# Half of the preceding item's down product between steps six and seven of gate and up, in an expert loop on one core

## The chip, the cores and the metric

One core of a Trainium2 chip runs the whole block. The metric is the device time of one execution in microseconds, lower is better; a kernel's time is the median of its runs. The profile is of one execution of its own.

## The reference

The reference is a decoder block: two attention branches that share one input projection, a gated merge, and then a sparse expert layer. The expert layer is what matters here:

```python
logits = (t @ w_router) + b_router          # 512 tokens, 32 experts
top_val, top_idx = lax.top_k(logits, 4)
gate = jax.nn.softmax(top_val, axis=-1)
# for each block of rows xb that chose expert e:
gu = xb @ w_gate_up[e] + b_gate_up[e]       # 1024 -> 2048
g, u = gu[:, :1024], gu[:, 1024:]
g = jnp.minimum(g, 7.0); u = jnp.clip(u, -7.0, 7.0)
a = (u + 1.0) * (g * jax.nn.sigmoid(1.702 * g))
y = a @ w_down[e] + b_down[e]               # 1024 -> 1024, times the gate, summed per token
```

Everything is float32. Each expert has 8 MB of gate and up weights and 4 MB of down weights.

## The kernel before

The first 420 us or so compute both attention branches, the merge and the routing. The rest is the expert layer, and the change lies there. An expert's rows make one **item**. Experts are ranked by how many tokens chose them: even items (0, 2, ..., 30) take up to 96 rows in 3 groups of 32, odd items up to 64 rows in 2 groups. The trace has 32 items. Item 0 and the last, item 31, stand outside the loop; a hardware loop `with pe.Fori(0, n_pairs) as pair` runs 15 times and does an odd item (`i` = 1) and an even item (`i` = 2) each time. I call one turn of it a **pair**.

Weights stream from HBM. SyncE issues six transfers of 2 MB for each item, in this order: gate and up in four parts, each for two of the eight steps (`gu_head` holds the first three parts, for steps 0 to 5, `gu_tail` the fourth, for steps 6 and 7), then down in two halves (`dn_even`, or `dn_odd0` and `dn_odd1`). There is one buffer for each gate and up part, so a part of the next item is only issued when TensorE is through with that part of this one (`gu_used`, and for the fourth part `bank_done`); the down weights have two sets of buffers, taken in turn, and each half is issued when the same half of the down product two items before is done (`dn_used`).

TensorE does for each item, in program order:

- `gate_up(i)` (L1816 to L1841): waits for `xT_ready` (the item's rows, transposed and scaled by VectorE) and for `gu_out` (VectorE has emptied the PSUM banks of the item before), then eight steps `k`, each waiting for its weights at even `k`, 4 products of 512 columns for each group (L1824). In even items the sums of earlier outputs into tokens (`pair_sums`, L1790) stand behind steps 1, 3, 5 and 6, and the first of them waits for `y_kept`.
- `lists(i + 2)` (L1770): a few small products for the token list of a later item.
- `down(i - 1)` (L1856 to L1874): the down product of the **preceding** item, in two halves `j`. It waits for `a_ready` (VectorE has written the activations `aT`) and `y_kept` (VectorE has taken the last down product out of PSUM).

A float32 product of the program stands as two matmul records in the trace: a half of an even item's down product is 16 + 8 products, 48 records.

VectorE's program order in each turn is fixed as well, and the prediction rests on it:

```python
pick(i + 2, later, pair)
if i == 2:
    for c in range(NB):
        add_sums(c, pair * 4 + (c + 1))
turn_out(i, pair)          # L1295: PSUM of gate and up -> act_gu
turn_rows(i + 1, pair)     # L1283, L1287: the next item's xT, then xT_ready
index(i + 2, pair)
keep_gates(i + 2, pair)
activate(i, e, pair)       # L1304 to L1314: ends in aT, a_ready
keep_low(i - 1, pair)      # L1323: y_lo, then y_kept
```

`turn_out` can only begin when `gate_up(i)` has filled a bank, at its last step. So between the end of `gate_up(i)` and the start of `gate_up(i + 1)`, VectorE empties PSUM and transposes the next item's rows, and TensorE does `lists` and `down(i - 1)`. GpSimd fetches the rows of a later item by an indirect DMA (L685) and ScalarE does the sigmoid (L905) and the first part of the output (`y_hi`, L912).

Of the kernel before, what the change touches and what calls it, by code (L numbers as in the profile page):

```python
# [56 lines left out]
def hybrid_block(nc, x, positions, norm1_g, w_in, b_forget, b_gate, q_norm_swa, k_norm_swa, sinks,  # L57
# [41 lines left out]
    with ExitStack() as ctx:  # L99
# [247 lines left out]
        def sem(name):  # L347
            return ctx.enter_context(nc.semaphore(name))
# [53 lines left out]
        a_ready = sem("a_ready")  # L402
        dn_used = [sem(f"dn_used{j}") for j in (0, 1)]
        y_high, y_kept, put_ready = sem("y_high"), sem("y_kept"), sem("put_ready")
        sums_ps, sums_added, out_done = sem("sums_ps"), sem("sums_added"), sem("out_done")
# [4 lines left out]
        def groups(i):  # L410
            return N_GROUPS - i % 2
# [7 lines left out]
        def counted(per_pair, at, pair):  # L419
            return at if pair is None else pair * per_pair + at  # L420
# [4 lines left out]
        def dn_chunk(i, j):  # L425
            return (dn_odd0, dn_odd1)[j][:, :] if i % 2 else dn_even[:, j, :]

        def gu_columns(k, j):
            return gu_chunk(k).rearrange("p (b n) -> p b n", b=4)[:, :, j * P:(j + 1) * P]

        def rows_of(i):

            return xT_odd[:, :, :] if i % 2 else xT[:, :, 0:groups(i) * GROUP]
# [1015 lines left out]
        def _(pe):  # L1449
# [313 lines left out]
            def lists(i, pair=None):  # L1763

                pe.wait_ge(sel_ready, counted(2, i + 1, pair))
                if i > 0:
                    pe.wait_ge(idx_ready, counted(2, i, pair))
                for a in (0,) if i % 2 else (0, 1):
                    for c in range(NB):
                        ins = pe.matmul(list_v[:, a, :], sel[:, c, a, :], row_now[:, c, :], start=(c == 0), stop=(c == NB - 1))  # L1770
                ins.then_inc(list_ps, 1)
# [11 lines left out]
            def sums(parts, c, n, banks=SUM_BANKS):  # L1783

                pe.wait_ge(sums_added, n)
                for at, (table, y) in enumerate(parts):
                    for half in (y_hi[y], y_lo[y]):
                        for h in (0, 1):
                            rows = slice(h * HD, (h + 1) * HD)
                            ins = pe.matmul(ps[:, banks, :][:, h], table[rows, c * P:(c + 1) * P], half[rows, :],  # L1790
                                            start=(at == 0 and half is y_hi[y]),
                                            stop=(at == len(parts) - 1 and half is y_lo[y]))
                return ins

            def pair_sums(c, pair, banks=SUM_BANKS, added=None):

                if c == 0:
                    pe.wait_ge(y_kept, pair * 2 + 2)
                    pe.wait_ge(put_ready, pair * 3 + 3)
                ins = sums(((put_odd, 2), (put_even, 0), (put_even_b, 1)), c, pair * 4 + ((c if added is None else added) + 1), banks)  # L1800
                ins.then_inc(sums_ps, 1)

            def bias_rows(h):

                pe.wait_ge(gateT_ready, 1)
                pe.wait_ge(gates_step, 1)
                pe.wait_ge(b_dn_in, 2 * 16 * NB)
                if h == 1:
                    pe.wait_ge(bdn_out, NB)
                for c in range(NB):  # L1810
                    pe.matmul(ps[:, BIAS_BANKS[c], :], gateT[c * E:(c + 1) * E, :], b_dn[h][c * E:(c + 1) * E, :],
                              start=True, stop=True).then_inc(bdn_ps, 1)

            def gate_up(i, pair=None, last=False):

                pe.wait_ge(xT_ready, counted(2, i + 1, pair))  # L1816
                if i > 0:
                    pe.wait_ge(gu_out, counted(2, i, pair))
                for k in range(KD):
                    if k % 2 == 0:  # L1820
                        pe.wait_ge(gu_in[k // 2], counted(32, i * 16 + 16, pair))
                    for n in range(groups(i)):
                        for j in range(4):
                            ins = pe.matmul(ps[j * GROUP:(j + 1) * GROUP, n, :], rows_of(i)[:, k, n * GROUP:(n + 1) * GROUP],  # L1824
                                            gu_columns(k, j), start=(k == 0), stop=(k == KD - 1))
                        if k == KD - 1:
                            ins.then_inc(bank_done, 1)
                    if k % 2 and k < KD - 1:
                        ins.then_inc(gu_used[k // 2], 1)
                    if i == 2 and k in SUM_STEPS:  # L1830
                        pair_sums(SUM_STEPS.index(k), pair)
                    if last and k == 3:
                        down(0, pair)
                    if last and k == 5:
                        pair_sums(0, pair)
                    if last and k == 6:
                        pair_sums(1, pair, LAST_BANKS[1], added=0)
                    if i == 0 and k == 1:
                        lists(1)
                    if i == 0 and k in (2, 5):  # L1840
                        bias_rows(k // 4)  # L1841
                    if i == 0 and k == 3:
                        extras()

            def extras():

                pe.wait_ge(extra_ready, 1)
                pe.wait_ge(gates_step, 3)
                for a, col in enumerate((x_expert, x_first, x_low)):
                    ins = pe.matmul(extra_ps[:, a, :], col[:, :].broadcast_to([E, P]), eyes[0:E, :], start=True, stop=True)  # L1850
                ins.then_inc(extra_ps_done, 1)

            def down(i, pair=None):

                pe.wait_ge(a_ready, counted(2, i + 1, pair))
                pe.wait_ge(y_kept, counted(2, i + 1, pair))  # L1856
                if i == 0:
                    pe.wait_ge(sums_added, counted(4, 1, pair))
                for j in (0, 1):
                    pe.wait_ge(dn_in[i % 2][j], counted(16, i // 2 * 16 + 16, pair))  # L1860
                    for k in range(4):
                        for u in range(4):
                            ins = pe.matmul(ps[u * GROUP:(u + 1) * GROUP, 5, :],  # L1863
                                            aT[:, 4 * j + k, u % 2 * GROUP:(u % 2 + 1) * GROUP],
                                            dn_chunk(i, j)[:, k * D + u // 2 * 512:k * D + (u // 2 + 1) * 512],
                                            start=(j == 0 and k == 0), stop=(j == 1 and k == 3))
                    if i % 2 == 0:
                        for k in (0, 2):
                            for u in range(4):
                                ku = k + u % 2  # L1870
                                ins = pe.matmul(ps[u * GROUP:(u + 1) * GROUP, 4, :], aT[:, 4 * j + ku, 2 * GROUP:],  # L1871
                                                dn_chunk(i, j)[:, ku * D + u // 2 * 512:ku * D + (u // 2 + 1) * 512],
                                                start=(j == 0 and k == 0), stop=(j == 1 and k == 2))
                    ins.then_inc(dn_used[j], 1)  # L1874
# [19 lines left out]
            ins.then_inc(gates0_ps, 1)  # L1894
            keep_warm(6)
            gate_up(0)
            lists(2)
            pe.wait_ge(items_ready, 1)
            n_pairs = pe.value_load(pairs[0:1, 0:1], min_val=PAIRS, max_val=MAX_PAIRS)
            with pe.Fori(0, n_pairs) as pair:  # L1900
                for i in (1, 2):
                    gate_up(i, pair)
                    lists(i + 2, pair)
                    down(i - 1, pair)
            gate_up(1, n_pairs, last=True)
            pair_sums(2, n_pairs, added=1)
            pair_sums(3, n_pairs, LAST_BANKS[1], added=2)
            down(1, n_pairs)
            pe.wait_ge(y_kept, n_pairs * 2 + 3)
            pe.wait_ge(put_ready, n_pairs * 3 + 4)  # L1910
# [25 lines left out]
```

## Time and profile before

| what | value |
|---|---|
| median of 3 runs | 1433.8 us (1432.73 to 1436.41) |
| the profiled execution's own time | 1432.87 us |
| its span | 1430.8 us |
| TensorE (PE) busy | 1363.6 us, 95% |
| VectorE (DVE) busy | 746.7 us, 52% |
| ScalarE (ACT), GpSimd (POOL) busy | 222.5 us, 191.0 us |
| weights' DMA queue q1 | 435.96 MB |
| DMA, HBM over the span | 312 GB/s |

The span runs from the first to the last instruction on record and is 2.1 us shorter than the execution's own time. Busy time of TensorE says little about how well it is used, as its matmuls are pipelined. The mean over the span also hides that the expert loop, from 447 us on, is a stage of its own, with other limits than the attention before it. In the views by window and in the timeline, times are microseconds from the start of the span.

### The profile page before, as it was taken

Reading aid. Unit: us, or ns where it says so; the run is one execution under the profiler, and the core shown is the slowest. Engines: PE = TensorE matmul, PEld = TensorE weight load, DVE = VectorE, ACT = ScalarE, POOL = GpSimd, SP = SyncE. Lnnn points to the kernel's source line nnn. Section 1 sums busy time; section 2 is a strip of 40 time slices with the busy share of each in tenths; the row PEclk is TensorE's granted clock in tenths of the full one; section 3 lists DMA queues with packets and bytes.
Section 4 is the critical chain, followed back from the end, with each engine's and each line's share of the span. In section 5 each row is a group of like instructions: output and inputs, shape, how many; then the busy total and the mean of one; then the engine's idle time right before and its main releaser. Section 6 shows DMA issues by size and latency. Waiting matters only on the chain.

```text
span 1430.8 us, 27506 instructions
## 1 busy us (share of the span) xinstructions
PE 1363.6 (95%) x11224; PEld 645.4 (45%) x11227; DVE 746.7 (52%) x1481; ACT 222.5 (16%) x415; POOL 191.0 (13%) x242
## 2 busy tenths in 40 slices
PE   6999999999989999999999999999899999999997
PEld 5888887778953333333232322323232332323233
DVE  5213736765257575454645444564544446565444
ACT  4224426642220000000000000000000000000000
POOL 2001400000002112021120202021020202112020
PEclk9999999999999999999999999999999999999999
DMA  6231320013679999999999999999999999999992
GB/s 192 88 117 61 114 91 1 2 34 120 245 301 368 409 395 416 404 414 414 409 413 397 418 406 414 415 410 415 392 418 407 409 414 415 417 399 417 402 413 116
DMA packets 59127, 447.27 MB, mean 313 GB/s; under 512 B 8592, under 2 KB 26032, under 8 KB 34480
## 3 DMA queue, kind: packets, MB, share of 16 engines
q1 hardware_dynamic: 55904, 435.96, 76.4%
q0 software_dynamic: 3072, 10.49, 2.3%
q8 instruction: 27, 0.44, 0.1%
q10 hardware_dynamic: 112, 0.28, 0.1%
q14 instruction: 12, 0.10, 0.0%
HBM read 442.51 MB, written 4.19 MB: 312 GB/s over the span
## 4 chain that ended last, share of the span: by engine, by line
PE 73%; DMA 19%; issue 4%; DVE 2%; ACT 1%; POOL 0%; SPq 0%; DVEq 0%; POOLq 0%; ACTq 0%
PE ps L1824 31%; DMA gu_head<-in_w_gate_up_dram 11%; PE ps L1863 10%; DMA gu_tail<-in_w_gate_up_dram 7%; PE ps L1790 7%; PE ps L1483 3%; PE ps L1485 3%; PE ps L1484 3%; PE ps L1871 2%; PE ps L1508 2%; PE ps L1509 2%; PE ps L1507 2%; PE ps L1474 1%; PE ps L1476 1%; PE ps L1475 1%
## 5 line engine op out<-in xcount | busy, mean ns | idle before, releaser
L1824 PE MATMUL ps<-gu_head,xT 128*32 128x512 f32 x2304 | 257.2, 594 | 3.0 <-DMA gu_head<-in_w_gate_up_dram 3.0
L1331 DVE TENSOR_TENSOR x_tok<-x_tok,ps 128x1024 f32<-128x1024 f32 x68 | 82.7, 1221 | 255.4 <-PE ps L1790 255.4
L1824 PE MATMUL ps<-gu_head,xT_odd 128*32 128x512 f32 x1536 | 168.5, 592 | 0.8 <-DVE act_gu L1295 0.6
L905 ACT ACTIVATE act_s<-act_gu 128x768 f32<-128x768 f32 (+1 forms) x32 | 23.6, 738 | 928.2 <-DVE act_gu L1306 893.5
L1824 PEld LDWEIGHTS ps<-gu_head,xT 128*32 128x32 f32 x2304 | 70.7, 110 | 169.5 <-issue 157.1
L1295 DVE STREAM_TRANSPOSE act_gu<-ps 128x512 f32<-128x512 f32 x80 | 57.2, 715 | 137.9 <-PE ps L1824 133.1
L685 POOL DMA_INDIRECT xg<-h_dram,idx_g x32 | 70.0, 2186 | 440.8 <-DVE row_all L1264 440.8
L942 DVE TENSOR_TENSOR st_l<-st_w,st_h 128x2048 fp32r<-128x2048 f32 x25 | 57.3, 2292 | 113.5 <-ACT st_h L749 113.5
L1863 PE MATMUL ps<-dn_even,aT 128*32 128x512 f32 x1024 | 116.1, 594 | 0.0
L1863 PE MATMUL ps<-dn_odd,aT 128*32 128x512 f32 x1024 | 113.2, 594 | 2.2 <-DVE aT L1314 2.2
L1824 PEld LDWEIGHTS ps<-gu_head,xT_odd 128*32 128x32 f32 x1536 | 49.3, 110 | 116.2 <-issue 110.7
L1824 PE MATMUL ps<-gu_tail,xT_odd 128*32 128x512 f32 x512 | 66.7, 666 | 29.4 <-DMA gu_tail<-in_w_gate_up_dram 29.4
L1824 PE MATMUL ps<-gu_tail,xT 128*32 128x512 f32 x768 | 88.8, 596 | 0.0
L1283 DVE STREAM_TRANSPOSE xT<-xg 32x256 f32<-32x256 f32 x180 | 77.7, 432 | 2.3
L1863 PEld LDWEIGHTS ps<-dn_odd,aT 128*32 128x32 f32 x1024 | 31.6, 110 | 70.0 <-issue 67.0
L1863 PEld LDWEIGHTS ps<-dn_even,aT 128*32 128x32 f32 x1024 | 31.7, 110 | 68.0 <-issue 67.6
L1871 PE MATMUL ps<-dn_even,aT 128*32 128x512 f32 x512 | 60.8, 592 | 0.0
L1283 DVE STREAM_TRANSPOSE xT_odd<-xg 32x256 f32<-32x256 f32 x128 | 55.1, 431 | 1.9 <-DMA xg<-h_dram,idx_g 0.4
L713 POOL COPY put_row<-row_all 128x1 f32 x15 | 2.8, 188 | 383.7 <-PE ps L1790 383.7
L749 ACT CAST st_h<-st_w 128x2048 fp32r<-128x2048 f32 x25 | 47.6, 1903 | 32.2 <-PE ps L1509 30.3
L1824 PEld LDWEIGHTS ps<-gu_tail,xT_odd 128*32 128x32 f32 x512 | 16.8, 120 | 77.3 <-DMA gu_tail<-in_w_gate_up_dram 40.5
L1483 PE MATMUL ps<-hT_h,st_h 128*128 128x512 f32 x128 | 50.0, 391 | 0.0
(373 smaller groups left out, 2009.6 us busy)
## 6 DMA issues: line engine op xcount, KB each, us to landing
gu_head<-in_w_gate_up_dram SPq DMA_DIRECT2D x96, 2048.0 KB, 22.4
gu_tail<-in_w_gate_up_dram SPq DMA_DIRECT2D x32, 2048.0 KB, 20.5
dn_even<-in_w_down_dram SPq DMA_DIRECT2D x32, 2048.0 KB, 25.1
dn_odd<-in_w_down_dram SPq DMA_DIRECT2D x32, 2048.0 KB, 21.5
st_w<-in_w_in_dram SPq DMA_DIRECT2D x17, 1024.0 KB, 5.3
st_w<-in_w_out_dram SPq DMA_DIRECT2D x4, 1024.0 KB, 5.1
x_tok<-in_x_dram SPq DMA_DIRECT2D x4, 512.0 KB, 6.2
st_w<-in_w_o_swa_dram SPq DMA_DIRECT2D x4, 512.0 KB, 3.5
```

The lines of the kernel that those rows point to most:

```text
L685: g.indirect_dma_start(out=xg[0:n, :], out_offset=None, in_=h2_dram[:, :], in_offset=bass.IndirectOffsetOnAxis(ap=idx_g[0:n, 0:1], axis=0) ...
L749: sc.copy(st_h[:, g % 2], st_w[:, g % 2]).then_inc(split_hi, 1)
L942: v.tensor_tensor(st_l[:, g % 2], st_w[:, g % 2], st_h[:, g % 2].bitcast(F32), ALU.subtract).then_inc(split_lo, 1)
L1283: ins = v.transpose(turned_rows[r, :, s].rearrange("r (k a) s -> r k a s", a=2), near[s, r].rearrange("s p k a -> s k a p"))
L1295: ins = v.transpose(act_gu[:, :, n * GROUP:(n + 1) * GROUP].rearrange("p (b k) s -> p b k s", k=4), ps[:, n, :].rearrange("p (b r k) -> p ...
L1331: v.tensor_tensor(x_tok[:, c, :].rearrange("p (h n) -> p h n", h=2), x_tok[:, c, :].rearrange("p (h n) -> p h n", h=2), ps[:, banks, :], A ...
L1483: pe.matmul(dst, wh[:, k], xh[:, k], start=(k == 0), stop=False)
L1484: pe.matmul(dst, wh[:, k], xl[:, k], start=False, stop=False)
L1790: ins = pe.matmul(ps[:, banks, :][:, h], table[rows, c * P:(c + 1) * P], half[rows, :], start=(at == 0 and half is y_hi[y]), stop=(at == l ...
L1824: ins = pe.matmul(ps[j * GROUP:(j + 1) * GROUP, n, :], rows_of(i)[:, k, n * GROUP:(n + 1) * GROUP], gu_columns(k, j), start=(k == 0), stop ...
L1863: ins = pe.matmul(ps[u * GROUP:(u + 1) * GROUP, 5, :], aT[:, 4 * j + k, u % 2 * GROUP:(u % 2 + 1) * GROUP], dn_chunk(i, j)[:, k * D + u // ...
L1871: ins = pe.matmul(ps[u * GROUP:(u + 1) * GROUP, 4, :], aT[:, 4 * j + ku, 2 * GROUP:], dn_chunk(i, j)[:, ku * D + u // 2 * 512:ku * D + (u ...
```

## The change

The down product is cut in its two halves. Inside the loop, `down(i - 1)`'s first half (`j` = 0, with its waits for `a_ready` and `y_kept`) is called from within `gate_up(i)`, behind step 5 and ahead of step 6; the second half stays where the whole stood, behind `lists`. The item after the loop (`last`) is as it was: the whole `down(30)` behind its step 3, and `down(31)` at the end.

```diff
                     if i == 2 and k in SUM_STEPS:
                         pair_sums(SUM_STEPS.index(k), pair)
+                    if pair is not None and not last and k == 5:
+                        down(i - 1, pair, (0,))
                     if last and k == 3:
                         down(0, pair)
...
-            def down(i, pair=None):
-
-                pe.wait_ge(a_ready, counted(2, i + 1, pair))
-                pe.wait_ge(y_kept, counted(2, i + 1, pair))
-                if i == 0:
-                    pe.wait_ge(sums_added, counted(4, 1, pair))
-                for j in (0, 1):
+            def down(i, pair=None, halves=(0, 1)):
+
+                if 0 in halves:
+                    pe.wait_ge(a_ready, counted(2, i + 1, pair))
+                    pe.wait_ge(y_kept, counted(2, i + 1, pair))
+                    if i == 0:
+                        pe.wait_ge(sums_added, counted(4, 1, pair))
+                for j in halves:
                     pe.wait_ge(dn_in[i % 2][j], counted(16, i // 2 * 16 + 16, pair))
...
                     gate_up(i, pair)
                     lists(i + 2, pair)
-                    down(i - 1, pair)
+                    down(i - 1, pair, (1,))
```

On TensorE, in the odd item of a pair: the gate and up steps are L1824, the list is L1770, and the down product of the even item before is L1863 and L1871 (L1866 and L1874 in the changed kernel); the ISA rows are its waits.

```order
+L1861 ISA
+L1863 ISA
+L1866 MATMUL ps<-dn_even,aT 32x512 x16
+L1874 MATMUL ps<-dn_even,aT 32x512 x8
 L1824 MATMUL ps<-gu_tail,xT_odd 32x512 x16
 L1765 REGISTER_ALU
 L1767 REGISTER_ALU
 L1770 MATMUL ps<-row_now,sel 128x5 x4
-L1858 ISA
-L1860 ISA
-L1863 MATMUL ps<-dn_even,aT 32x512 x16
-L1871 MATMUL ps<-dn_even,aT 32x512 x8
```

The first 24 products of the down product, and both of its waits, moved from behind the list to ahead of the steps that read `gu_tail`. The next 24 follow the list in both kernels.

On TensorE, at the end of the even item of a pair, before the change (the last rows ahead of the loop's branch):

```order
L1824 MATMUL ps<-gu_tail,xT 32x512 x12
L1765 REGISTER_ALU
L1770 MATMUL ps<-row_now,sel 128x5 x8
L1863 MATMUL ps<-dn_odd_207,aT 32x512 x16
L1863 MATMUL ps<-dn_odd_206,aT 32x512 x16
```

and with the change:

```order
L1824 MATMUL ps<-gu_tail,xT 32x512 x12
L1765 REGISTER_ALU
L1770 MATMUL ps<-row_now,sel 128x5 x8
L1866 MATMUL ps<-dn_odd_206,aT 32x512 x16
```

One half of the odd item's down product is left between the end of the even item's gate and up and the start of the next odd item's; the other stands ahead of step 6, behind the third of the sums. VectorE, ScalarE, GpSimd and SyncE keep their order.

## Rows read from the trace of the kernel before

**Rows 1.** The page: busy time of the engines; the DMA share in 40 slices.
```profile
PE 1363.6 (95%) x11224; PEld 645.4 (45%) x11227; DVE 746.7 (52%) x1481; ACT 222.5 (16%) x415; POOL 191.0 (13%) x242
DMA  6231320013679999999999999999999999999992
```

**Rows 2.** The chain of waits: starts of odd items' gate and up (start, us, what).
```profile
446.94 13.94 PE ps L1824 x128
...
506.32 13.73 PE ps L1824 x128
...
565.50 13.73 PE ps L1824 x128
...
624.68 3.48 PE ps L1824 x32
...
1380.17 6.87 PE ps L1824 x64
```

**Rows 3.** Windows: length, busy time of the engines, granted clock, DMA share, GB/s.
```profile
506.30:565.50 59.20, 59.20 (x548) 19.61 (x540) 33.50 (x68) 3.32 (x5) 9.54 (x8) 1.00 1.00 405
...
1001.20:1064.00 62.80, 59.22 (x544) 19.17 (x536) 33.01 (x68) 3.32 (x5) 9.06 (x8) 1.00 1.01 408
...
1190.00:1254.40 64.40, 61.68 (x552) 19.94 (x548) 34.04 (x68) 3.32 (x5) 10.07 (x8) 0.97 1.01 414
```

**Rows 4.** Waits, 624 to 1380 us: us in total, times, longest us.
```profile
PE ps L1824 <- DMA gu_tail<-in_w_gate_up_dram: 29.4, 12, 3.2
...
PE ps L1824 <- DMA gu_head<-in_w_gate_up_dram: 3.0, 7, 0.4
```

**Rows 5.** Timeline of TensorE in one pair: start, us, instructions [idle before].
```profile
520.18 3.64 PE L1863 MATMUL ps<-dn_even,aT 128*32 128x512 f32 x32
...
525.35 3.62 PE L1863 MATMUL ps<-dn_even,aT 128*32 128x512 f32 x32
...
530.50 5.33 PE L1824 MATMUL ps<-gu_head,xT 128*32 128x512 f32 x48
...
535.76 0.50 PE L1790 MATMUL ps<-y_hi,put_odd 64*128 64x512 f32 x2
...
558.43 7.08 PE L1863 MATMUL ps<-dn_odd,aT 128*32 128x512 f32 x64
565.32 1.04 PE L1824 MATMUL ps<-gu_head,xT_odd 128*32 128x512 f32 x8
```

**Rows 6.** Timeline of VectorE in the same pair.
```profile
510.43 0.74 DVE L1323 SCALAR_TENSOR_TENSOR y_lo<-ps,gate_all,y_hi 128x512 fp32r<-128x512 f32 x1
...
520.77 5.33 DVE L1283 STREAM_TRANSPOSE xT<-xg 32x256 f32<-32x256 f32 x12
526.14 0.96 DVE L1287 TENSOR_TENSOR xT<-xT,g_near 128x768 f32<-128x768 f32 x1
...
532.26 1.41 DVE L1323 SCALAR_TENSOR_TENSOR y_lo<-ps,gate_all,y_hi 128x512 fp32r<-128x512 f32 x2
...
558.92 3.54 DVE L1283 STREAM_TRANSPOSE xT_odd<-xg 32x256 f32<-32x256 f32 x8
562.50 0.69 DVE L1287 TENSOR_TENSOR xT_odd<-xT_odd,g_near 128x512 f32<-128x512 f32 x1
```

**Rows 7.** Timeline of TensorE: three waits for `gu_tail`, and what followed.
```profile
762.91 5.34 PE L1824 MATMUL ps<-gu_tail,xT_odd 128*32 128x512 f32 x32 [3.13 <-DMA gu_tail<-in_w_gate_up_dram]
...
825.92 3.64 PE L1824 MATMUL ps<-gu_tail,xT_odd 128*32 128x512 f32 x32 [1.92 <-DMA gu_tail<-in_w_gate_up_dram]
...
888.76 5.34 PE L1824 MATMUL ps<-gu_tail,xT_odd 128*32 128x512 f32 x32 [2.70 <-DMA gu_tail<-in_w_gate_up_dram]
```

**Rows 8.** Timeline of VectorE and TensorE near the end: a wait for `y_lo`.
```profile
1420.90 0.75 DVE L1323 SCALAR_TENSOR_TENSOR y_lo<-ps,gate_all,y_hi 128x512 fp32r<-128x512 f32 x1 [5.87 <-ACT y_hi L912]
...
1421.88 0.50 PE L1790 MATMUL ps<-y_hi,put_odd 64*128 64x512 f32 x2 [1.98 <-DVE y_lo L1323]
```

**Rows 9.** Transfers of `gu_tail` from issue to landing: item 0's; the 24 from 624 us on.
```profile
DMA to landing us min/median/max: 7.6/7.6/7.6
...
DMA to landing us min/median/max: 19.0/23.1/27.4
```

## The prediction, before the changed kernel was run

> **What bounds the kernel now.** I read the page first. TensorE is busy 95% of the span, VectorE 52% [rows 1], and the DMA digits stand at 9 from the fourteenth slice to the last but one. So two resources look full in the expert loop, and the page doesn't say which one sets the pace. The chain of waits does, if one measures the distance between starts of odd items. The reader is to see that the first full pairs take 59.18 us each (506.32 to 565.50 to 624.68), and that the twelve pairs from 624.68 to 1380.17 take 62.96 us each [rows 2]. In a fast pair TensorE has no idle time at all, 59.20 us busy in a window of 59.20 us [rows 3]: 59.18 us is TensorE's own work. In the later ones it waits for weights, 29.4 us for `gu_tail` and 3.0 us for `gu_head` [rows 4]. The windows show the DMA share at 1.00 and 1.01, with 405 to 414 GB/s, in the fast pairs and in the slow ones alike [rows 3]. So the queue needs 62.96 us for a pair. At first it falls behind and lives on what was loaded ahead; from 624 us on **the queue sets the pace**, at 3.78 us a pair above TensorE's work. Over all 15 pairs TensorE would need 59.38 (the first) + 14 x 59.18 = 887.9 us. They take 933.2 us (446.94 to 1380.17). The difference, 45.3 us, is what the queue costs: 32.4 us of waits and the rest mostly a lower clock behind some of them (below).
>
> **What the change removes.** The wait for `gu_tail` in the odd item stands right where half of the even item's down product now goes, and that half lasts 5.17 us (520.18 to 525.35) [rows 5]. The waits were 3.2 us at most [rows 4]. So this wait is filled, and the drops of the clock behind it go as well. By itself this is worth little: the queue moves the same bytes in the same order and is full all the time, so a wait filled at step 6 comes back at the next transfer. It doesn't bring the queue's 62.96 us down.
>
> **What the change adds.** The whole down product used to stand between one item's gate and up and the next. Under it VectorE emptied PSUM and transposed the rows of the next item, for which the next gate and up waits. I look at what is left of that cover, in the pair at 506 us, where nothing waits for DMA.
>
> - Odd to even item. The down product begins at 520.18; half of it ends at 525.35, where the whole ended at 530.50 [rows 5]. VectorE's transposes of `xT` run from 520.77, and the scaling behind them ends at 526.14 + 0.96 = 527.10 [rows 6]. They can't come sooner: they follow `turn_out`, which needs the last step of gate and up, and their order on VectorE isn't changed. A **new wait of 1.75 us** for `xT_ready`.
> - Even item's first sums. They stand behind steps 0 and 1, 5.26 us behind the start of gate and up (530.50 to 535.76) [rows 5], so at 527.10 + 5.26 = 532.36 now. They wait for `y_kept`, and `y_lo` ends at 532.26 + 1.41 = 533.67 [rows 6]. That chain hangs on VectorE's order (the transposes, then the activations, then `keep_low`), which begins at the end of gate and up as before. A **second wait of 1.31 us**.
> - Even to odd item. The down product of the odd item takes 6.89 us (558.43 to 565.32) [rows 5]; half of it ends at 561.88. `xT_odd` is ready at 562.50 + 0.69 = 563.19 [rows 6]. A **third wait of 1.31 us**.
>
> Together 4.37 us a pair. An end on VectorE isn't a start on TensorE: `y_lo` ended at 1421.65 and TensorE began at 1421.88 [rows 8], 0.23 us later. The first wait's delay is swallowed by the second, so two of them count, each between nothing and 0.23 us; I take half, 0.25 us together. So 4.62 us a pair, with bounds of 4.37 and 4.83 from these rows. The waits could be smaller than that if VectorE ran faster beside an idle TensorE, for which no row speaks; I let them go down to 4.0.
>
> **What lies beside other work.** The first half's own waits cost nothing: in the odd item `y_lo` ends at 511.17 [rows 6], 4.85 us behind the start of gate and up at 506.32 [rows 2]; that start moves 2.1 us ahead of VectorE (half a down product of 3.45 us less the wait of 1.31 us), so 7.0 us, and six steps take 10.3 us (four take 6.87 us in the last item [rows 2]). In the last item `down(30)` stands behind four steps, 6.87 us, against those 7.0 us: 0.2 us more, once. On SyncE nothing changes its place. The reload of `gu_tail` is issued half a down product later, and the first half of the down weights right behind it, when its buffer has long been free; a transfer took 7.6 us on an empty queue [rows 9], and from the end of one gate and up to step 6 of the next there are over 20 us (3.45 + 1.3 + 10.3 + 5.17). That cover is gone only if the queue is full.
>
> **The sum.** TensorE's pace becomes 59.18 + 4.62 = 63.8 us a pair, 0.84 us above what the queue needs. So the queue's waits all go, and VectorE's take their place: 15 x 4.62 = 69.3 us come, 45.3 us go, 0.2 us at the end. Net +24.2 us. On the profiled execution's 1432.87 us that gives **1457 us**. The median shown is 0.9 us above that execution, far inside my range, and I add nothing for it.
>
> **The rivals.** A. *The queue goes on setting the pace, no change.* If VectorE's waits came to less than 3.78 us a pair, they would only fill time in which TensorE waited for weights. The pair stays at 62.96 us, and the time at 1432 to 1436 us, not slower. The point that decides is 3.78 us, and my sum is 0.84 us above it; a shorter chain on VectorE by 20% would do it. For it speaks the DMA share of 1.01 [rows 3]. The Trainium skill, page "Perfetto Trace Analysis", section "Identifying the Most-Contended Engine", says to find the most contended engine and to work on that one first, and to judge DMA by the bandwidth it reaches. By that rule DMA is the one here and a new order on TensorE would change nothing, 1433 us. Against it speaks that VectorE, at 52%, isn't loaded, yet what counts is the 6.9 us from the end of gate and up to `xT`, not its share. 11%.
>
> B. *The clock falls as well.* Behind waits of 3.13 and 2.70 us the next 32 matmuls took 5.34 us instead of 3.64 us, 1.7 us more; behind one of 1.92 us they didn't [rows 7], and the granted clock of such a window is 0.97 [rows 3]. My new waits are 1.75 us and less, but three of them stand in each pair, two of them 5.3 us apart. The Trainium skill, "TensorE: Matmul & The Clock Gate", section "What's actually happening", says that the gate goes by how busy the array has been recently, so their closeness may count. One fall in every second pair costs 7 x 1.7 = 12 us, 1469 us; one in each, 1482 us. 8%.
>
> C. *The queue runs dry and stays late.* `gu_tail` is issued up to 5.17 us later, and with a pace only 0.84 us above the queue's a lost microsecond isn't won back. If the 19.0 us and more of a full queue [rows 9] met the 20 us window with some scatter, a wait of 1 us in each pair would give 1472 us. 5%.
>
> D. *Faster by over 0.3%.* The filled wait and the missing falls of the clock would have to count and VectorE's chain not. 3%; about 1428 us.
>
> **How the numbers follow.** My forecast has 73%. A measurement of this kernel can tell about 0.3%, 4.3 us, from no change; with B and C, slower has 0.86, same 0.11 (A), faster 0.03 (D). From waits of 4.0 us a pair (9 us less than my sum, 1448 us) and some scatter I go down to 1444 us; upward, 4.83 us gives 1460 us, and half of B and of C takes it to 1470 us. Outside lie A and D and the dearer halves of B and C, together 2 in 10.
>
> **What would show it.** In the profile after, pairs of one length from the first on, near 63.8 us. TensorE waits for `xT` or `xT_odd` of VectorE (L1287) about 1.8 and 1.4 us, in all 30 starts, and for `y_lo` (L1323) about 1.3 us at the first sums of the even items. No wait for `gu_tail`; a granted clock of 1.00 in the loop; DMA below 410 GB/s, and transfers of `gu_tail` that land sooner than 19 us. The forecast is wrong if pairs stay at 63.0 us with waits for weights (A), or if VectorE's chain behind a gate and up is shorter than 6.9 us.

## The result, and the profile after

The changed kernel takes 1458.0 us, the median of 4 runs (1457.6 to 1459.6), against 1434.3 us before. The ratio is 1.0177, with a 95% interval of 1.0162 to 1.0192. The forecast was 1457 us, slower, in a range of 1444 to 1470 us.

The page of the profiled execution, same parts as in [rows 1]:

```profile
span 1457.5 us, 27506 instructions
...
PE 1358.6 (93%) x11224; PEld 650.5 (45%) x11227; DVE 745.2 (51%) x1481; ACT 220.8 (15%) x415; POOL 190.7 (13%) x242
...
DMA  6232320014589899999999999999999999999991
```

The page would not have told what happened. TensorE lost 2 points of busy share, VectorE is at 51%, and the DMA digits still stand at 9.

The chain of waits, starts of odd items' gate and up (compare [rows 2]):

```profile
448.67 10.51 PE ps L1824 x96
...
512.52 10.51 PE ps L1824 x96
...
576.36 10.51 PE ps L1824 x96
...
1342.45 10.51 PE ps L1824 x96
...
1406.29 7.07 PE ps L1824 x64
```

Every pair takes 63.84 us from the first on; there is no fast beginning and no slow rest. The 15 pairs take 957.6 us (448.67 to 1406.29), against 933.2 us. Of the 26.7 us by which the span grew, 24.4 us lie in the loop, 1.7 us ahead of it and 0.6 us behind it. (The chain gives a start without a wait 0.18 us later than the timeline does: 1380.17 against 1379.99 us for the last item before. By the timeline it is 24.6 us in the loop and 0.4 us behind it, and the prediction's 59.38 us for the first pair is 59.20 us.) Eight other kernels of this study, with the same code ahead of the loop, entered it anywhere from 445.6 to 448.8 us, so the 1.7 us lie within the scatter.

The waits of TensorE over the loop (us in total, times, longest us), where [rows 4] showed DMA:

```profile
PE ps L1824 <- DVE xT L1287: 25.3, 15, 1.7
PE ps L1824 <- DVE xT_odd L1287: 20.2, 15, 1.4
PE ps L1790 <- DVE y_lo L1323: 17.2, 15, 1.2
```

TensorE waits three times in each pair, always for VectorE, and nowhere in the loop for a weight. One pair of TensorE's timeline (compare [rows 5]):

```profile
512.52 10.51 PE L1824 MATMUL ps<-gu_head,xT_odd 128*32 128x512 f32 x96 [1.34 <-DVE xT_odd L1287]
...
531.73 3.64 PE L1866 MATMUL ps<-dn_even,aT 128*32 128x512 f32 x32
...
538.77 5.36 PE L1824 MATMUL ps<-gu_head,xT 128*32 128x512 f32 x48 [1.68 <-DVE xT L1287]
545.27 0.50 PE L1790 MATMUL ps<-y_hi,put_odd 64*128 64x512 f32 x2 [1.15 <-DVE y_lo L1323]
...
571.37 3.64 PE L1866 MATMUL ps<-dn_odd,aT 128*32 128x512 f32 x32
```

The idle times shown, 1.68, 1.15 and 1.35 us (from the next start at 576.36), sum to 4.2 us, but the pair grew by 4.66 us. Starts show why. The half at 531.73 is followed by gate and up 7.04 us later, where 5.17 us would be the distance without a wait: 1.87 us lost, 1.68 of them shown as idle. Likewise 6.50 against 5.26 us (1.24 lost), and 4.99 against 3.45 us (1.54 lost). Together 4.65 us. Some 0.1 to 0.2 us of each wait (0.19, 0.09 and 0.19 us here) is hidden under the modelled end of the last matmul. **Losses are read from distances between starts, not from the idle times.**

VectorE's timeline in that pair (compare [rows 6]):

```profile
532.31 5.33 DVE L1283 STREAM_TRANSPOSE xT<-xg 32x256 f32<-32x256 f32 x12
537.68 0.96 DVE L1287 TENSOR_TENSOR xT<-xT,g_near 128x768 f32<-128x768 f32 x1
...
543.63 1.40 DVE L1323 SCALAR_TENSOR_TENSOR y_lo<-ps,gate_all,y_hi 128x512 fp32r<-128x512 f32 x2
```

`xT` is ready at 538.64, 6.91 us behind the start of the down half at 531.73; before it was 527.10 - 520.18 = 6.92 us. `y_lo` ends at 545.03, 13.30 us behind it, before 13.49 us. VectorE's chain up to `xT` is what it was, and `y_lo` comes 0.2 us sooner; TensorE now arrives ahead of both.

The window of that pair (compare [rows 3]), and the transfers of `gu_tail` from issue to landing, 624 to 1370 us ([rows 9]):

```profile
512.50:576.40 63.90, 59.70 (x544) 19.85 (x546) 33.40 (x69) 3.20 (x5) 9.49 (x7) 1.00 1.01 406
```
```profile
DMA to landing us min/median/max: 7.5/12.0/17.2
```

The granted clock is 1.00. The share of DMA is 1.01 as before, although the queue holds nobody up. The landings tell the two apart: 19.0 us at least and 23.1 us in the median before; now 7.5 us at least, as on an empty queue, and 12.0 us in the median.

### The profile page after: what moved, and what is told of

It is laid out like the page before. It is cut to its first block, busy times and chain, and to the rows that moved or that the text cites. A ratio compares the mean times of both kernels' runs of the same rounds, so it can differ in the third digit from the quotient of the medians.

```text
span 1457.5 us, 27506 instructions
## 1 busy us (share of the span) xinstructions
PE 1358.6 (93%) x11224; PEld 650.5 (45%) x11227; DVE 745.2 (51%) x1481; ACT 220.8 (15%) x415; POOL 190.7 (13%) x242
## 4 chain that ended last, share of the span: by engine, by line
PE 73%; DVE 16%; issue 7%; ACT 2%; DVEq 1%; DMA 1%; POOL 0%; SPq 0%; ACTq 0%; POOLq 0%
PE ps L1824 33%; PE ps L1866 8%; PE ps L1790 7%; DVE xT L1283 5%; DVE xT_odd L1283 4%; PE ps L1483 3%; PE ps L1484 3%; PE ps L1485 3%; PE ps L1874 2%; PE ps L1509 2%; PE ps L1507 2%; PE ps L1508 2%; DVE act_gu L1304 1%; PE ps L1474 1%; PE ps L1476 1%
## 5 line engine op out<-in xcount | busy, mean ns | idle before, releaser
L1824 PE MATMUL ps<-gu_head,xT 128*32 128x512 f32 x2304 | 257.3, 594 | 25.3 <-DVE xT L1287 25.3
L1824 PE MATMUL ps<-gu_head,xT_odd 128*32 128x512 f32 x1536 | 168.3, 593 | 20.9 <-DVE xT_odd L1287 20.2
L1824 PEld LDWEIGHTS ps<-gu_head,xT 128*32 128x32 f32 x2304 | 70.6, 110 | 193.4 <-issue 192.9
L1866 PE MATMUL ps<-dn_odd,aT 128*32 128x512 f32 x1024 | 116.3, 595 | 2.2 <-DVE aT L1314 2.2
L1866 PE MATMUL ps<-dn_even,aT 128*32 128x512 f32 x1024 | 116.2, 594 | 0.2 <-issue 0.2
L1824 PEld LDWEIGHTS ps<-gu_head,xT_odd 128*32 128x32 f32 x1536 | 50.1, 110 | 138.1 <-issue 138.1
L1824 PE MATMUL ps<-gu_tail,xT 128*32 128x512 f32 x768 | 88.5, 594 | 0.0
L1866 PEld LDWEIGHTS ps<-dn_even,aT 128*32 128x32 f32 x1024 | 32.3, 110 | 67.8 <-issue 67.4
L1874 PE MATMUL ps<-dn_even,aT 128*32 128x512 f32 x512 | 60.9, 592 | 0.0
L1866 PEld LDWEIGHTS ps<-dn_odd,aT 128*32 128x32 f32 x1024 | 30.1, 109 | 66.5 <-issue 63.6
L1824 PE MATMUL ps<-gu_tail,xT_odd 128*32 128x512 f32 x512 | 58.2, 592 | 0.0
L1790 PE MATMUL ps<-y_hi,put_odd 64*128 64x512 f32 x136 | 33.5, 487 | 19.2 <-DVE y_lo L1323 19.2
```

Source lines behind the costliest of these rows:

```text
L1866: ins = pe.matmul(ps[u * GROUP:(u + 1) * GROUP, 5, :], aT[:, 4 * j + k, u % 2 * GROUP:(u % 2 + 1) * GROUP], dn_chunk(i, j)[:, k * D + u // ...
```

## The experiments

The theory is that of **two paces**: a pair takes the longer of what the queue needs (62.96 us) and of TensorE's own 59.18 us plus its waits for VectorE. Over the whole loop the queue needs less than 15 x 62.96 us, since it starts with a lead: before, the loop took 933.2 us, 45.3 us above TensorE's 887.9 us. So it is the total of VectorE's waits over the loop that has to pass 45.3 us, 3.0 us a pair; 3.78 us a pair is the point only once the lead is gone. The theory's rivals: each wait for VectorE is paid on top of before (additive); and the harm is not VectorE's but that `gu_tail` is reloaded later (late reload).

**One early half alone.** In the first kernel only the odd item has its early half, in the second only the even item.

```diff
-                    if pair is not None and not last and k == 5:
+                    if pair is not None and not last and i == 1 and k == 5:
...
-                    down(i - 1, pair, (1,))
+                    down(i - 1, pair, (1,) if i == 1 else (0, 1))
```

> The early half in the odd item alone (the even item's down product). Theory, two paces: a pair takes the longer of the queue's 62.96 us and TensorE's 59.18 us plus the waits for VectorE. Here only the waits for xT and y_lo are left, 1.68 + 1.17 us in the changed kernel's trace and about 0.3 us of starts, so 62.3 us: below the queue. The time stays at 1432 to 1437 us, and waits for weights remain. Rival, additive (each wait for VectorE is paid on top of before): 15 x 2.85 = 43 us would come on top and the wait for gu_tail would go, net 1445 to 1460 us. Rival, late reload (the queue suffers since gu_tail is issued 5.2 us later): the same 5.2 us stand here, so about half of the 24 us or more.

Measured: 1435.0 us against 1433.3 us, ratio 1.0013 (1.0002 to 1.0025), within what was expected. The waits over the loop and the first and last odd item in the chain:

```profile
PE ps L1824 <- DVE xT L1287: 25.3, 15, 1.7
PE ps L1790 <- DVE y_lo L1323: 17.2, 15, 1.2
```
```profile
446.33 10.51 PE ps L1824 x96
...
1380.91 6.87 PE ps L1824 x64
```

42.5 us of waits for VectorE stand on TensorE, and the time is that of before. Each of the 15 pairs takes 62.3 us, as forecast. The additive rival, at least 1445 us, falls, and so does the late reload, which would have cost half of the 24 us or more. I had expected waits for weights to remain, and there are none: the fast pairs of before used up in three pairs the weights that had been loaded ahead, some 11 us of them (3 x 3.78); at 62.3 us a pair that lead melts by 0.66 us a pair, 9.9 us in all, and lasts to the end. So the pace here is never the queue's; it is TensorE's with 3.1 us of waits a pair. That its sum, 934.6 us, is nearly the 933.2 us of before comes from the size of the waits: 3.1 us is just above the 3.0 us that the queue cost a pair on average.

> The early half in the even item alone (the odd item's down product). Theory, two paces: TensorE's pace is 59.18 + 1.35 + 0.1 = 60.6 us, 2.3 us below the queue's 62.96 us: the time stays at 1432 to 1437 us, with the waits for gu_tail in the odd item as before or a little shorter. Rival, additive: 15 x 1.35 = 20 us on top, 1450 us or more. Rival, late reload: the reload of gu_tail for the odd item is issued 3.4 us later and its need isn't put off here, so the wait for it grows by 3.4 us where the queue isn't what holds it: up to 1485 us.

Measured: 1437.5 us, ratio 1.0020 (1.0009 to 1.0030). This is 1 to 4 us slower, just above the 1432 to 1437 us expected. The waits:

```profile
PE ps L1824 <- DVE xT_odd L1287: 20.2, 15, 1.4
...
PE ps L1824 <- DMA gu_head<-in_w_gate_up_dram: 11.4, 11, 1.3
PE ps L1824 <- DMA gu_tail<-in_w_gate_up_dram: 9.0, 12, 1.5
```

The first pair takes 61.6 us, with a wait of 0.70 us for `gu_tail`, the next three 60.7 to 61.0 us, about as the theory has it, and the later ones 62.7 to 63.5 us with waits for weights: the queue again. The additive rival, 1450 us or more, falls. That the waits for `gu_tail` shrank (29.4 us before), and the time didn't rise to 1485 us, speaks against the late reload. What the 1 to 4 us are was not tried.

So each early half alone costs nearly nothing, both together 24 us. The waits add up (3.1 and 1.5 us a pair alone, 4.65 us together), the costs don't: what counts is by how much the waits' sum passes 3.0 us a pair. 15 x (4.65 - 3.02) = 24.4 us is what the loop lost; with 3.78 us as the point it would have lost only 13 us.

**VectorE's chain taken off the path.** VectorE turns the next item's rows while gate and up still runs:

```diff
-                        for c in range(NB):
-                            add_sums(c, pair * 4 + (c + 1))
-                    turn_out(i, pair)
+                        add_sums(0, pair * 4 + 1)
+                        add_sums(1, pair * 4 + 2)
                     turn_rows(i + 1, pair)
+                    if i == 2:
+                        add_sums(2, pair * 4 + 3)
+                        add_sums(3, pair * 4 + 4)
+                    turn_out(i, pair)
```

> The changed kernel, and on VectorE the next item's rows are turned ahead of turn_out (in the even item between the second and third sum), so while gate and up still runs. Theory, two paces: xT is ready before the early start, the waits for xT and xT_odd go, y_lo comes some 3.6 us sooner and its wait goes too; TensorE's pace falls to 59.2 us and the queue's 62.96 us rules again: 1430 to 1436 us. Rival, late reload: VectorE has nothing to do with it, the time stays near 1458 us. Rival, additive: without VectorE's waits the filled wait for gu_tail counts, 29 us less than before, 1405 us.

Measured: 1436.4 us, ratio 1.0011 (0.9995 to 1.0027), the same as before and 0.4 us above the range expected. The late reload (near 1458 us) falls, as `gu_tail` is still reloaded late here, and so does the additive rival (1405 us). The three waits for VectorE are gone from the loop; what is left but for one of 0.6 us at its entry is DMA, now at the start of the even item:

```profile
PE ps L1827 <- DMA gu_head<-in_w_gate_up_dram: 30.3, 11, 4.7
```
```profile
656.39 7.05 PE L1827 MATMUL ps<-gu_head,xT 128*32 128x512 f32 x48 [4.59 <-DMA gu_head<-in_w_gate_up_dram]
```

The wait for `gu_tail` is filled, as the change means to do, and comes back three transfers on (two halves of down weights lie between), for `gu_head`, in larger pieces: 4.59 us of idle time, and the next 48 matmuls take 7.05 instead of 5.36 us, at a granted clock of 0.76 over that stretch (part of it at the lower level, 1.2 GHz, and the rest at 2.4 GHz). This is the step of the prediction that a filled wait is worth little while the queue sets the pace.

> The same order on VectorE, with the down product whole as before. Theory: VectorE was hidden under the whole down product, nothing of it was on the path, and the queue rules: 1432 to 1436 us, the waits for gu_tail of about 2.5 us as before. Rival (the new order on VectorE is of use, or does harm, by itself): a time that differs from before by over 4 us.

Measured: 1435.8 us, ratio 1.0016 (1.0002 to 1.0031), within the range. The new order on VectorE does nothing by itself, since the whole down product covered it. One detail of the expectation was off: most of the waits for weights stand at `gu_head` (25.2 us) and fewer at `gu_tail` (10.4 us), so where the queue's lateness shows depends on small shifts. The sum doesn't.

**The queue made lighter.** In the loop each half of the down weights is loaded to half of its columns, 1 MB instead of 2 MB. These kernels leave out work and don't compute the reference; they are for timing alone.

```diff
-                        load_dn(e, i, j)
+                        sp.dma_start(dn_chunk(i, j)[:, 0:2 * D], w_dn_v[bass.ds(e, 1), j].rearrange("a p n -> (a p) n")[:, 0:2 * D]).then_inc(dn_in[i % 2][j], 16)
```

> Before, but in the loop each half of the down weights is loaded to half of its columns only (1 MB instead of 2 MB; the rest of the buffer keeps older weights), so the queue has 4 MB less to move for each pair. Theory, two paces: the queue's need falls from 62.96 to some 53 us a pair, below TensorE's 59.18 us, and all waits for weights go: 45 us less, 1386 to 1391 us. Rival (TensorE or the order of its work sets the pace and the waits are a matter of latency): less than 20 us less, over 1414 us.

> The changed kernel with the same lighter loads. Theory, two paces: its pace of 63.84 us is TensorE's with the waits for VectorE, the queue isn't in it: 1455 to 1459 us, no change from the changed kernel, so 69 us above the run with the old order and light loads. Rival, late reload (the queue runs dry and gu_tail comes late): lighter loads help, 1440 us or less.

> The changed kernel with VectorE's rows turned first and with the light loads of the down weights (half of their columns). Theory: once VectorE's chain is off the path and the queue is light, the early halves cost TensorE nothing: pairs of 59.2 us as in the light run of the old order, 1387 to 1393 us. Rival (the early half costs TensorE something by itself, by its place between steps): over 1400 us.

| kernel, light loads | median us | ratio to before (95%) | pairs, us |
|---|---|---|---|
| old order | 1389.4 | 0.9687 (0.9666 to 0.9709) | 59.2, all 15 |
| changed order | 1458.1 | 1.0177 (1.0155 to 1.0200) | 63.8 to 63.9, all 15 |
| changed order, rows turned first | 1389.7 | 0.9692 (0.9673 to 0.9711) | 59.2, all 15 |

The chain of the old order with light loads, first and last odd item, then the window at 512 us of the old and of the changed order:

```profile
447.48 13.94 PE ps L1824 x128
...
1335.38 6.87 PE ps L1824 x64
```
```profile
512.50:576.40 63.90, 63.90 (x588) 21.04 (x584) 34.43 (x71) 3.32 (x5) 9.51 (x7) 1.00 0.95 364
```
```profile
512.50:576.40 63.90, 59.72 (x548) 19.87 (x544) 33.42 (x68) 3.21 (x5) 9.56 (x8) 1.00 0.88 339
```

The old order gains 45 us with a lighter queue (by the ratio; 43 us against the median of 1432.6 us taken with it), the 45.3 us at which the prediction put the queue's cost, and its 15 pairs take 887.9 us, the number worked out there. The changed order gains nothing at all: its pace is not the queue's. That ends the late reload, which a queue with 14% fewer bytes (373 of 436 MB) would have helped, and no transfer is needed to explain the 24 us. The difference between the first two lines, 69 us, is the full price of the waits for VectorE (forecast 69.3 us). The third line shows that the early halves themselves cost TensorE nothing.

**A longer chain on VectorE.** One more operation stands ahead of the scaling of the rows, into a scratch tile:

```diff
+                v.tensor_scalar(extra_w[:, :, :], bc(g2_near[:, :], 2, SLOTS), 1.0, None, ALU.mult)
                 dve.wait_ge(x_raw, counted(2, i + 1, pair))
```

> Before, with one more VectorE operation of 768 columns (to a scratch tile) between the transposes and the scaling of the next item's rows: VectorE's chain is d = about 0.5 to 1 us longer. Theory: the whole down product covers it (3.4 us to spare in the odd item, 2.1 us in the even one): no change, 1432 to 1437 us.

> The changed kernel with the same extra operation. Theory: both chains of VectorE are on the path in every pair (xT and y_lo share one, xT_odd is the other), so the time grows by 2 x 15 x d: 15 us for d of 0.5 us, 29 us for 0.96 us, that is 1473 to 1487 us. Rival, late reload: VectorE isn't on the path, 1458 us.

Measured: the old order 1434.5 us, ratio 1.0004 (0.9989 to 1.0019); the changed order 1475.4 us, 17.4 us above the changed kernel. VectorE and TensorE in the latter, one pair:

```profile
601.41 0.56 DVE L1287 TENSOR_SCALAR extra_w<-g_near 128x768 f32<-128x768 f32 x1
601.89 0.95 DVE L1289 TENSOR_TENSOR xT<-xT,g_near 128x768 f32<-128x768 f32 x1
```
```profile
537.78 7.00 PE L1826 MATMUL ps<-gu_head,xT 128*32 128x512 f32 x48 [2.15 <-DVE xT L1289]
...
602.97 5.36 PE L1826 MATMUL ps<-gu_head,xT 128*32 128x512 f32 x48 [2.15 <-DVE xT L1289]
```

The operation puts off the scaling by 0.48 us (601.41 to 601.89), and most pairs grow from 63.84 to 64.8 us, by nearly twice 0.48 us: 14 us over the loop. The old order doesn't feel it, and not only because the queue covers it: its first three pairs, in which nothing waits for weights, take 59.2 us as before. In the changed order the loop grew by 15.7 us. What is above the 14 us is in the two rows of TensorE: behind two waits of 2.15 us each the matmuls took 7.00 us once (granted clock 0.76 over 7 us) and 5.36 us the other time (1.00). Four pairs had such a fall of the clock and took 65.2 or 65.3 us. Another fall, in the last down product behind the loop, cost 1.7 us in this trace; kernels without the extra operation show it at that place as well, in some traces and not in others.

**What the gathers cost the queue.** Each gather in the loop fetches 16 rows instead of 64 or 96, so this kernel doesn't compute the reference either:

```diff
-                gather(1)
+                gather(1, 16)
...
-                gather(2)
+                gather(2, 16)
```

> Before, with each gather in the loop cut to 16 rows (of 64 or 96; the other rows keep what an earlier gather left). Of the queue's 62.96 us a pair, 12 x 4.89 = 58.7 us are weights by the spacing of their landings, so the two gathers, 160 rows, cost 4.3 us. Theory: the cost goes with the rows, a fifth is left, the queue needs 59.5 us, and nearly all waits for weights go: 1388 to 1398 us. Rival (a gather's cost is fixed, or the queue isn't what sets the pace): 1425 us or more.

Measured: 1393.0 us, ratio 0.9716 (0.9696 to 0.9736). The first nine pairs take 59.2 us, the last ones 60.1 us, where the lead is used up:

```profile
1217.97 10.48 PE L1824 MATMUL ps<-gu_head,xT_odd 128*32 128x512 f32 x96
...
1278.03 10.48 PE L1824 MATMUL ps<-gu_head,xT_odd 128*32 128x512 f32 x96
```

So the queue needs 60.1 us a pair with 32 gathered rows and 62.96 us with 160: 22 ns for each of the 128 rows left out; expected were 59.5 us. The rival, 1425 us or more, falls. All gathers together move 10.5 MB of 447 MB before, and leaving out four fifths of the loop's rows saves the old order some 40 us.

No kernel here that computes the whole reference beats the one before. The old order with light loads and with short gathers shows where the next gain is: in the queue, by fewer or cheaper gathered rows, and not in TensorE's order. A cheaper gather that still fetches all rows was not tried.

## Why the prediction was right

- *The queue sets the pace before, TensorE's own work is 59.18 us a pair.* Shown: with light loads the old order takes 59.2 us in every pair and loses 45 us.
- *Filling the wait for `gu_tail` is worth little.* Shown by the run with the rows turned first: the wait moves to `gu_head`, the time stays.
- *Three new waits, 1.75, 1.31 and 1.31 us, 4.37 us by the rows and 4.62 us with the delay between engines.* Measured as losses 1.87, 1.24 and 1.54 us, 4.65 us. The forecast of 63.8 us a pair met 63.84 us. It held because VectorE's chain was measured from the end of gate and up, and up to `xT` that chain didn't change (6.92 us before, 6.91 us after). That it held to 0.03 us is luck in part: the delay from the end on VectorE to the start on TensorE was not half of 0.23 us but all of it (`y_lo` ended at 545.03 and TensorE began at 545.27; the third wait lost 0.23 us more than 1.31), and `y_lo` came 0.19 us sooner, which took most of that back. Why it came sooner was not traced.
- *45.3 us of the queue's waits go, 69.3 us come, 0.2 us at the end.* In the loop 24.4 us came, forecast 24.0 us. At the end it was 0.4 us by the timeline, twice the forecast. All of it lies ahead of `down(30)`, where the wait was foreseen: that product starts 7.26 us behind the last item's start, before 6.86 us. The trace names no releaser for it, but `y_lo` ended at 1413.21, 6.92 us behind the last item's start (foreseen were 7.0 us), and `down(30)` began 0.34 us after that. The last item's start and `down(30)` before, then `down(30)` after:

```profile
1379.99 7.05 PE L1824 MATMUL ps<-gu_head,xT_odd 128*32 128x512 f32 x64
1386.85 3.62 PE L1863 MATMUL ps<-dn_even,aT 128*32 128x512 f32 x32
```
```profile
1413.55 3.64 PE L1866 MATMUL ps<-dn_even,aT 128*32 128x512 f32 x32 [0.18 <-issue]
```

- *The first half's waits for `aT` and `y_kept` cost nothing in the loop, the late reload nothing either.* No such wait is in the trace of the loop, and light loads change nothing.
- *Rival A, no change.* It asked for waits under 3.78 us a pair. "No change" is what happens when only one half is early: 3.1 us and 1.5 us. But its point was wrong: it left out the lead, which the prediction's own sum had in (45.3 us over 15 pairs, 3.0 us a pair). Waits of 3.78 us would already have cost 11 us, so the change lay 1.6 us beyond the point and not 0.84 us, and A was less likely than its 11% by this argument. Nor would a chain shorter by 20% have been needed to reach 3.78 us: the waits would have to shrink by 18%, and as 0.48 us more on both chains cost nearly 0.96 us a pair, 0.42 us less on each, 6% of 6.9 us, would do. The advice of the Trainium skill, page "Perfetto Trace Analysis", section "Identifying the Most-Contended Engine", to work on the most contended engine first, holds for the old order, where less DMA gains 45 us. That a new order on TensorE would change nothing was the prediction's own inference from it and doesn't hold: the new order made a chain of waits the bound, on an engine that is 51% busy.
- *Rival B, the clock falls as well.* Not behind the changed kernel's waits of 1.68 us and less: its granted clock is 1.00 over the loop. With the longer chain on VectorE, behind waits of 2.15 us, it fell in 4 of 15 pairs and cost 0.4 us in each of them and not 1.7 us, since the slower steps ran in what was the wait for `y_lo`.
- *Rivals C and D* didn't occur.
- *A small misreading.* The DMA digits stand at 9 from the thirteenth slice on, not the fourteenth; nothing hangs on it.

## What to carry to other kernels

Before moving work on an engine, ask what that work covers where it stands now: here a down product of 10.3 us hid a 6.9 us chain on an engine that is 52% busy, the 5.2 us left of it didn't, and the share told nothing of it. Where two resources are both near the limit, compute the total of each over the loop, with what was loaded ahead; waits on the faster one cost nothing until they pass the difference of the totals (45.3 us here, 3.0 us a pair), and what is beyond costs in full, which also means that two harmless halves can make a harmful whole. A wait that is filled while a saturated queue sets the pace comes back a few transfers later.

## What was not expected

- With full loads the DMA share reads 1.00 to 1.01 whether the queue sets the pace or not. The median time of `gu_tail` from issue to landing tells: 23.1 us before, 22.2 and 19.0 us in the kernels with only the even item's half early and with the rows turned first, where the queue sets the pace; 12.0 us after, where it doesn't. The minimum is a worse sign (12.3 us with the rows turned first).
- The rows of the gathers cost the queue 22 ns each, some 2.9 us a pair for 128 rows of 4 KB, which is 0.5 MB; at the 4.9 us between landings of 2 MB transfers of weights in the trace of before (893.6 and 898.5 us, for one) the same bytes would take 1.2 us. Why a gathered row costs more than twice its share stays open.
- Behind a wait of 2.15 us the clock fell in some pairs and not in others, with the same work before it. The wait's length alone doesn't decide here: in the trace of before it fell behind 2.70 us and not behind 3.17 us.
